# Fourteen matmuls whose results nobody reads, in TensorE's two pauses between the router's logits and the gather of the first expert's tokens

## The reference, cut to what matters

```
x = x + einsum('bsm,md->bsd', mixed, w_out)
h = rms_norm(x, norm2_w)
logits = einsum('bsd,de->bse', h, w_router)        # 256 x 16
aff = softmax(logits, axis=-1)
gate, idx = lax.top_k(aff.transpose(0, 2, 1), 32)  # per expert: 32 tokens
xin = h[idx]                                       # gather
hid = silu(xin @ w_gate[e]) * (xin @ w_up[e])      # 1024 x 1024 each
y = (hid @ w_down[e]) * gate
x = x + zeros.at[idx].add(y)                       # scatter
```

## Time and profile before

| | before |
|---|---|
| median of three runs | 1692.85 us |
| profiled execution, its own time | 1688.29 us |
| its span, first to last instruction | 1686.5 us |
| mean granted TensorE clock | 0.938 |
| TensorE busy | 1608.4 us, 95% |
| VectorE busy | 761.2 us, 45% |
| ScalarE busy | 676.4 us, 40% |
| HBM read over the span | 398.23 MB, 237 GB/s |

### The profile page before, as it was taken

The page is one execution under the profiler, slowest core; times in us unless marked ns, Lnnn a source line. Parts: engine busy times, 40 slices in busy tenths (PEclk is TensorE's granted clock), DMA queues, the critical chain, the costliest instruction groups (busy, mean ns, idle before and its releaser), DMA issues.

```text
span 1686.5 us, 26658 instructions
## 1 busy us (share of the span) xinstructions
PE 1608.4 (95%) x11006; PEld 1331.8 (79%) x11006; DVE 761.2 (45%) x1006; ACT 676.4 (40%) x741; POOL 46.8 (3%) x37
## 2 busy tenths in 40 slices
PE   7996879999999989999999999999999999999998
PEld 7885755555554544799999889999899989899997
DVE  4679531111111111554446755444644456754443
ACT  5573331212121212543444754343643454754343
POOL 0006200000000000000000000000000000000000
PEclk9897977878787888999999999999999999999999
DMA  7632479999999999665555436564565546346552
GB/s 233 178 100 76 171 324 428 427 428 428 428 429 428 428 429 429 213 222 176 192 179 165 135 109 218 175 198 150 177 199 174 196 128 213 112 155 194 177 192 80
DMA packets 164072, 400.17 MB, mean 237 GB/s; under 512 B 5753, under 2 KB 136233, under 8 KB 151593
## 3 DMA queue, kind: packets, MB, share of 16 engines
q1 hardware_dynamic: 162824, 397.74, 64.1%
q10 hardware_dynamic: 1184, 1.57, 0.3%
HBM read 398.23 MB, written 1.06 MB: 237 GB/s over the span
## 4 chain that ended last, share of the span: by engine, by line
PE 82%; DMA 6%; DVE 6%; ACT 3%; issue 2%; POOL 0%; SPq 0%; DVEq 0%; ACTq 0%; POOLq 0%
PE ps L563 12%; PE ps L565 12%; PE ps L564 12%; PE ps L795 10%; PE ps L588 6%; PE ps L589 6%; PE ps L590 6%; PE ps L783 4%; PE ps L803 4%; DMA ring<-w_expert_up 4%; PE ps L844 3%; DMA ring<-w_in 2%; PE ps L534 1%; PE ps L525 1%; ACT w1h_sb L1073 1%
## 5 line engine op out<-in xcount | busy, mean ns | idle before, releaser
L1715 DVE TENSOR_TENSOR wl_sb<-raw_sb,wh_sb 128x2048 fp32r<-128x2048 f32 x162 | 370.9, 2292 | 295.1 <-ACT wh_sb L1213 294.8
L563 PE MATMUL ps<-xTh_sb,wh_sb 128*128 128x256 f32 x1696 | 482.2, 284 | 1.5 <-DVE xTl_sb L1403 1.5
L564 PE MATMUL ps<-xTl_sb,wh_sb 128*128 128x256 f32 x1696 | 479.9, 283 | 0.0
L565 PE MATMUL ps<-xTh_sb,wl_sb 128*128 128x256 f32 x1696 | 479.9, 283 | 0.0
L1213 ACT ACTIVATE wh_sb<-raw_sb 128x2048 fp32r<-128x2048 f32 x162 | 309.9, 1915 | 300.0 <-PE ps L565 186.4
L563 PEld LDWEIGHTS ps<-xTh_sb,wh_sb 128*128 128x128 f32 x1696 | 325.3, 192 | 5.6 <-DVE xTl_sb L1403 3.6
L564 PEld LDWEIGHTS ps<-xTl_sb,wh_sb 128*128 128x128 f32 x1696 | 325.4, 192 | 1.9 <-issue 0.5
L565 PEld LDWEIGHTS ps<-xTh_sb,wl_sb 128*128 128x128 f32 x1696 | 325.4, 192 | 0.0
L795 PE MATMUL ps<-ring,work 128*32 128x512 f32 x1152 | 155.7, 693 | 6.0 <-DMA ring<-w_expert_up 5.9
L588 PE MATMUL ps<-wh_sb,hidh_sb 128*128 128x512 f32 x384 | 151.2, 394 | 1.2 <-DVE wl_sb L1715 1.2
L589 PE MATMUL ps<-wl_sb,hidh_sb 128*128 128x512 f32 x384 | 149.9, 390 | 0.0
(11 more groups left out here) (294 smaller groups left out, 1846.7 us busy)
## 6 DMA issues: line engine op xcount, KB each, us to landing
ring<-w_expert_gate SPq DMA_DIRECT2D x24, 2048.0 KB, 20.8
ring<-w_expert_up SPq DMA_DIRECT2D x24, 2048.0 KB, 21.7
ring<-w_expert_down SPq DMA_DIRECT2D x24, 2048.0 KB, 27.8
raw_sb<-ffn_gate SPq DMA_DIRECT2D x44, 1024.0 KB, 5.3
raw_sb<-ffn_up SPq DMA_DIRECT2D x44, 1024.0 KB, 5.3
raw_sb<-ffn_down SPq DMA_DIRECT2D x44, 1024.0 KB, 4.9
raw_sb<-w_in SPq DMA_DIRECT2D x22, 1024.0 KB, 5.4
ring<-w_in SPq DMA_DIRECT2D x16, 1024.0 KB, 5.7
```

The costliest lines, as they stand in the source:

```text
L563: pe.matmul(to, w_h[:, k, fs], x_h[:, k, :], start=k == 0, stop=False)
L564: pe.matmul(to, w_h[:, k, fs], x_l[:, k, :], start=False, stop=False)
L565: mm = pe.matmul(to, w_l[:, k, fs], x_h[:, k, :], start=False, stop=k == KD - 1)
L1715: dve.tensor_tensor(wl[j], raw[j], wh[j].bitcast(F32), ALU.subtract).then_inc(raw_free[j], 1)
```

## The change

A helper `stay_busy(count)` issues `count` matmuls of the identity with a 128x512 piece of `xn` into PSUM bank 4; nothing waits for them and nothing reads their results. Twelve are issued after the transposes of the affinities, ahead of the wait for `place_done`; two after the transposes of the places, ahead of the waits for `tb_rows_done` and `hot_done`. A wait for `xn_done` is added ahead of the transposes of the affinities; it is issued a second time at its old place, as before.

```
+            def stay_busy(count):
+
+                for _ in range(count):
+                    pe.matmul(bank(4), ident, xn[:, 0, LEFT], start=True, stop=True)
+
             turn_norm(1, True, 4)
...
             pe.wait_ge(sem["aff_done"], 1)
+            pe.wait_ge(sem["xn_done"], 2)
             for t in range(TT):
                 mm = pe.transpose(bank(5)[0:NE, t * P:t * P + P], aff[:, t, :], ident)
             mm.then_inc(sem["affT_ps"], 1)
+            stay_busy(12)
             pe.wait_ge(sem["place_done"], 1)
             for t in range(TT):
                 mm = pe.transpose(bank(6)[:, t * NE:t * NE + NE], place[:, t * P:t * P + P], ident[0:NE, 0:NE])
             mm.then_inc(sem["placeT_ps"], 1)
+            stay_busy(2)
```

## The result

| | before | after |
|---|---|---|
| median of 15 runs each, side by side | 1689.69 us | 1694.02 us |
| ratio, 95% interval | | 1.0022 (1.0014 to 1.0030) |
| profiled execution, its own time | 1688.29 us | 1694.02 us |
| its span | 1686.5 us | 1692.2 us |
| granted clock, mean | 0.938 | 0.940 |

Slower by 4.3 us by the medians, 3.7 by the ratio (2.4 to 5.1 by its interval); the forecast was 3.6. The time that was forecast, 1696.5 us, is 2.5 above the measured 1694.02, because it was counted on the first three runs of the kernel before. Their median was 1692.85; the 15 runs lie in two heaps, nine from 1687.8 to 1689.9 and six from 1692.6 to 1693.7, and their median is 1689.69.

What follows compares the result with a forecast made beforehand. Saturated expert transfers bound the kernel, starting when the first expert's first product ends. Gather start 6.6 late, minus 3.3 from a faster gather, plus 0.3 on the product: +3.6 us, 1692.85 to 1696.5; range 1690.5 to 1701.5.

Steps and rivals of the forecast that it cites:

- The bound, and what moves it: Router to experts' end: saturated transfers, 432 us, start when the first expert's first product ends; its shift moves the end.
- The price of a matmul: Each added matmul: two records, 0.86 us at the high clock; a record takes 0.86 us low, 0.43 high.
- Rival D: Added matmuls in both pauses cost half as much, one record each; -1.9 to -4.2 us, faster; chance 0.08.
- The twelve: First pause, behind the affinities' transposes: added matmuls take 12.4 us, clock rising after 4.2; places' transposes move to 236.7.
- The two: Second pause, behind the places' transposes: 1.72 us against 1.43 before; the gather starts 6.6 us late.
- The gather: First gather, ahead of the first product: 3.74 us at the high clock instead of 7.01, 3.3 us back.
- The first product: First expert's first product, behind the gather: wholly at the low clock, 3.85 us to the issue against 3.59, 0.3 lost.
- Rival B: First expert's first product: the clock holds high through it, so only +1.3 us, 1694.2; chance 0.12.
- The sum: First transfer issue and end: 6.6 - 3.3 + 0.3 = +3.6 us, 1692.85 becomes 1696.5, slower by 0.21%.
- C: First pause: the clock doesn't rise under the added matmuls, 20.6 us; +16.6 us, 1709.5; chance 0.05.
- E: Experts' stretch: the transfers' later start doesn't carry to the end; its spread, 1694 to 1699, is inside the forecast's 0.70.
- the same: Whole kernel: chance 0.57 that the time changes by no more than about 0.3%, 5 us.

Runs made afterwards that it cites:

- narrow: The changed kernel with thirteen and two added matmuls of 32 columns instead of twelve and two of 512; ratio 1.0008 to the kernel before.
- the work in the experts: The kernel before with two dense matmuls at the head of one expert in four and none in the two pauses; ratio 1.0009 to the kernel before.
- twelve, two and one: The changed kernel with one more dense matmul behind the first gather; ratio 1.0008 to the kernel before.
- first twelve-only: The changed kernel without the two matmuls in the second pause, first of two measurements; ratio 1.0036 to the kernel before, 1.0033 when repeated.
- Four and one: The changed kernel with four matmuls instead of twelve in the first pause and one instead of two in the second; ratio 0.9979 to the kernel before.
- four, one and one: The changed kernel with four matmuls in the first pause, one in the second and one behind the first gather; ratio 0.9972 to the kernel before.
- three, one and one: The changed kernel with three matmuls in the first pause, one in the second and one behind the first gather; ratio 0.9990 to the kernel before.
- twenty-four: The changed kernel with twenty-four matmuls instead of twelve in the first pause, the two kept; ratio 1.0088 to the kernel before.

## Why the prediction was right, point by point

**The bound, and what moves it.** Right. Change of A in the profile, and change of the end by the ratio: -5.1 and -4.7, -3.3 and -3.5, -0.5 and -1.7, 0.0 and +1.4 (narrow, undecided), +2.6 and +1.7, +4.7 and +3.7, +15.0 and +14.9, and for the work in the experts 0.0 and +1.5 (undecided). Two fit badly: twelve, two and one with +4.0 and +1.4, and the first twelve-only with +2.9 and +6.1 (the second has +6.1 and +5.6). A is read from one execution and the end from 6 to 15, each ratio with 1.4 to 3.3 us either way, and B moves besides.

**The price of a matmul.** 0.86 us at the high level was right (24 instead of 12: 10.3 us more). Rival D is out.

**The twelve.** Forecast 12.4 us, measured 13.2 in the changed kernel's profile: the clock rose 5.6 us after they began, at 229.3, later than the longest of the three rows I bounded it by (2.9, 4.2, 5.4). Over the profiles the twelve took 11.6 to 13.3. This is the term that was mis-sized: the delay is not a property of the operation, as my choice of the residual's row took it to be. The same operation in the same place saw the rise after 2.3 to 5.6 us, depending on the execution. I also let the twelve start 0.2 us behind the affinities' transposes; it was 0.4.

**The two.** From the places' transposes to the gather 2.04 us against 1.43; I had 1.8. Together the gather starts 7.8 us late, not 6.6.

**The gather.** 3.65 against a forecast of 3.74: 3.4 back, against 3.3 forecast. Four and one shows this gain by itself. That the clock holds because dense matmuls stand right ahead of the gather is only argued: with two of them there it held in all three profiles (3.65 us), with one it held in two (3.73) and was lost in three, one and one (5.78).

**The first product.** At the low level, 3.9 us to the issue against 3.59, +0.3: right to a tenth. Rival B didn't occur, and four, one and one shows what it would have taken, 2.2 us to the issue.

**The sum.** 7.8 - 3.4 + 0.3 = +4.7 at the first issue instead of +3.6. The end came to +3.7 to +4.3. So the forecast of the end is better than its terms, and that it hit the ratio's 3.7 to a tenth is luck. The absolute time would have pointed to the wrong mechanism: rival B's 1694.2 is nearer to the measured 1694.02 than the forecast's 1696.5, only because the base was 3.2 us too high. The first product's rows decide it, and they show the low level.

**What was wrong.** "What happens to TensorE's clock after it is worth little." B runs from 446.2 to 450.5 us over the profiles, as much as the change itself. I had allowed 1.8 us for it. The reason that I gave, "because TensorE waits for transfers anyway", holds only in the last experts: from the first issue at 244.24 to 581.00 no transfer keeps it waiting in the kernel before, and behind the last wait there is no transfer left to hide its clock, 21.3 to 24.6 us of work in ten profiles. "The stretch's length is fixed by bytes" is right up to the last wait and no further. B's spread would explain a good part of the scatter of the runs before, which lie in two heaps 4 to 5 us apart; that each heap has its own B is argued, not shown.

**Rivals.** C (no rise) is out by the clock's rows, E (air in the stream) by twenty-four. The prediction took about 0.3% for the least that can be told from no change, and gave "the same" 0.57. The interval here, 1.0014 to 1.0030, tells 0.22% from nothing, so that bound was too wide.

## What to carry to other kernels

Work put in to hold TensorE's clock pays only if it fits the pause, priced at the level at which it starts: here a pause of 6 us takes four matmuls of 128x512 in float32, and only just (4.8 us in one profile, 6.3 in another), and twelve cost more than the clock gives back. Putting dense work into each short pause on the way, right up to the stage that shall have the clock, gave the best kernel here, but it is no guarantee: with three instead of four the clock fell in the gather. Look for the one event the bottleneck waits for (here the product that frees the first transfer): what moves that event counts in full. What comes behind it is at best free within the slack there, 7.5 us here, and the work behind the last wait is not hidden at all. One profile isn't enough where the clock's edges fall differently each time; compare lengths between events, not absolute times.

## What the runs showed of the hardware

Being busy was not enough to raise TensorE's clock or to hold it. 26 narrow records filling 5.6 us left it at 0.50. Gathers without a gap, begun at the high level, lost it in their middle in three of the profiles (at 242.6, 241.4 and 231.4, in 4.20, 5.89 and 5.78 us instead of 3.65). Dense float32 matmuls begun at 0.50 saw the rise after about 2.3 us (226.67 to 229.0, first twelve-only profile) up to 5.6 us (223.69 to 229.3, changed kernel). The late start of the saturated queue (427 GB/s before) was paid in full: with A 10.3 us longer than in the changed kernel, B stayed the same, 448.06 against 448.04, and the last wait for a transfer ended 425.06 us behind the first issue against 425.04.
